# Weight tiles placed 256 bytes instead of 32 bytes off the activations' alignment in each SBUF partition

## What is computed

```python
u = rmsnorm(x, norm_mix) * (1.0 + scale1) + shift1
aq, ak, av, bq, bkv, biq, bik, biw, cq, ck, cv, g = split_cols(u @ w_in)
...
merged = gates[:, :, 0] * y_a + gates[:, :, 1] * y_b + gates[:, :, 2] * y_c
x = x + gate1 * (merged @ w_o)
u2 = rmsnorm(x, norm_mlp) * (1.0 + scale2) + shift2
h = jnp.square(jax.nn.relu(u2 @ w_ff1))
x = x + gate2 * (h @ w_ff2)
x = rmsnorm(x, norm_final)
for layer in range(2):
    proj = rms_norm(x, pre_norm[layer]) @ w_in_2[layer]
    ...
    mix = concatenate([y_conv, y_ret])
    x = x + rms_norm(mix @ w_out[layer], post_norm[layer])
```

## The kernel before

| tile | address | modulo 512 |
|---|---|---|
| u_hi, u_lo | 24704, 32896 | 128 |
| raw | 41088 | 128 |
| w_hi, w_lo | 73888, 90272 | 160 |
| h_hi, h_lo, mix_hi, mix_lo, m, oa, ob, oc | 146528 and on | 96 |

## Time and profile before

### The profile page before, as it was taken

How to read it: one execution, slowest core, us unless ns; L and a number is a source line. 1 busy time by engine, 2 the same in 40 slices (tenths; PEclk the granted TensorE clock), 3 DMA queues, 4 the chain that set the end, 5 groups by cost and what they waited for, 6 DMA issues and landing times.

```text
span 1012.1 us, 22089 instructions
## 1 busy us (share of the span) xinstructions
PE 971.3 (96%) x7850; PEld 946.8 (94%) x7850; DVE 611.2 (60%) x1032; ACT 493.8 (49%) x811; POOL 714.9 (71%) x902
## 2 busy tenths in 40 slices
PE   6998999999889999999999999999999999999997
PEld 6898889998889999999899999999989999999996
DVE  4889996656877554322555567764154666676612
ACT  3545557654446554454354446444435444644441
POOL 1585666668669888777466668998746666799873
PEclk9999999999999999999899999999999999999999
DMA  9984554646445547554244444455513444445521
GB/s 374 381 311 174 203 200 181 244 139 263 150 158 172 203 166 276 181 194 166 89 161 167 166 164 169 166 188 191 204 42 141 152 165 166 162 173 192 186 100 42
DMA packets 28226, 185.23 MB, mean 183 GB/s; under 512 B 3028, under 2 KB 5505, under 8 KB 6273
## 3 DMA queue, kind: packets, MB, share of 16 engines
q1 hardware_dynamic: 25832, 167.93, 46.2%
q10 hardware_dynamic: 2328, 16.40, 4.4%
HBM read 183.26 MB, written 1.07 MB: 182 GB/s over the span
## 4 chain that ended last, share of the span: by engine, by line
PE 82%; DVE 11%; issue 4%; ACT 2%; DMA 1%; POOL 0%; SPq 0%; POOLq 0%; DVEq 0%; ACTq 0%
PE mm L548 24%; PE mm L549 23%; PE mm L550 23%; PE mm L580 3%; DVE score L1573 1%; PE mm L566 1%; DVE w_lo L1382 1%; PE ps_s L877 1%; PE mm L567 1%; PE mm L568 1%; DVE ada_raw L1423 1%; PE ps_o L892 1%; PE ps_o L928 1%; DMA ident<-ident_d 1%; DVE merged L1720 1%
## 5 line engine op out<-in xcount | busy, mean ns | idle before, releaser
L464 POOL TENSOR_TENSOR w_lo<-raw,w_hi 128x256 fp32r<-128x256 f32 x876 | 700.1, 834 | 253.3 <-ACT w_hi L979 253.3
L548 PE MATMUL mm<-u_hi,w_hi 128*128 128x256 f32 x1608 | 464.3, 289 | 2.0 <-issue 1.8
L549 PE MATMUL mm<-u_lo,w_hi 128*128 128x256 f32 x1608 | 452.5, 281 | 0.0
L550 PE MATMUL mm<-u_hi,w_lo 128*128 128x256 f32 x1608 | 452.3, 281 | 0.0
L979 ACT ACTIVATE w_hi<-raw 128x1024 fp32r<-128x1024 f32 x291 | 308.2, 1059 | 165.7 <-PE mm L550 162.7
L548 PEld LDWEIGHTS mm<-u_hi,w_hi 128*128 128x128 f32 x1608 | 303.8, 189 | 8.4 <-issue 7.8
L549 PEld LDWEIGHTS mm<-u_lo,w_hi 128*128 128x128 f32 x1608 | 303.9, 189 | 2.0 <-issue 1.9
L550 PEld LDWEIGHTS mm<-u_hi,w_lo 128*128 128x128 f32 x1608 | 303.8, 189 | 0.0
L1382 DVE TENSOR_TENSOR w_lo<-raw,w_hi 128x1024 fp32r<-128x1024 f32 x72 | 96.9, 1346 | 117.8 <-ACT w_hi L979 116.1
L548 PE MATMUL mm<-mix_hi,w_hi 128*128 128x256 f32 x256 | 72.2, 282 | 0.4 <-DVE mix_lo L1957 0.4
L549 PE MATMUL mm<-mix_lo,w_hi 128*128 128x256 f32 x256 | 72.0, 281 | 0.0
(11 more groups left out here) (285 smaller groups left out, 1314.9 us busy)
## 6 DMA issues: line engine op xcount, KB each, us to landing
raw<-weights SPq DMA_DIRECT2D x145, 1024.0 KB, 4.8
ada_raw<-ada ACTq DMA_DIRECT2D x14, 1024.0 KB, 4.9
ada_raw<-ada SPq DMA_DIRECT2D x6, 1024.0 KB, 12.5
ada_more<-ada SPq DMA_DIRECT2D x4, 1024.0 KB, 12.6
bias<-tab_scratch SPq DMA_DIRECT2D x1, 1536.0 KB, 9.5
dec<-decay ACTq DMA_DIRECT2D x1, 1536.0 KB, 7.3
x<-xT SPq DMA_DIRECT2D x1, 1024.0 KB, 9.8
out<-x SPq DMA_DIRECT2D x4, 256.0 KB, 2.2
```

The source lines that it names most:

```text
L464: ins = nc.gpsimd.tensor_tensor(w_lo[:, s, at], r[:, at], hi[:, at], ALU.subtract)
L548: nc.tensor.matmul(dst, wh, rhs_hi(k), start=a, stop=False)
L549: nc.tensor.matmul(dst, wh, rhs_lo(k), start=False, stop=False)
L550: i = nc.tensor.matmul(dst, wl, rhs_hi(k), start=False, stop=b)
```

## The change

The two unused tiles step_w and step_vec get 64 columns instead of 8, that is 256 bytes instead of 32.

```diff
     raw = keep("raw", [P, RAW_PAIRS, 2 * KC * P])
-    keep("step_w", [P, 8])
+    keep("step_w", [P, 64])
     w_hi = keep("w_hi", [P, SLOTS, KC * P], F32R)
     w_lo = keep("w_lo", [P, SLOTS, KC * P], F32R)
-    keep("step_vec", [P, 8])
+    keep("step_vec", [P, 64])
     vec = keep("vec", [P, N_COLS])
```

## The result

| | us |
|---|---|
| before, median of 6 runs | 1009.33 (1007.19 to 1010.97) |
| after, median of 6 runs | 1018.38 (1015.86 to 1018.77) |
| ratio | 1.0089, 95% interval 1.0072 to 1.0107 |
| profiled execution after, its span | 1018.77, 1016.9 |

The forecast was 1010.8 us, no change. The time rose by 9.05 us; the new median, 1018.38, lies inside the range from 982 to 1037 and near the lower price of rival B (1019.4).

A forecast was written before the change was run, and what follows sets the result against it. TensorE was taken as the bound, matmuls times step; all terms were 0, so the profiled 1014.07 us, lying 3.25 above the median, gave 1010.8 us, range 982 to 1037.

The forecast's parts named there:

- rival B: Matmuls on u: reads meeting mid-matmul delay the next; +8.6 us (1019.4) or +25.3 (1036.1); chance 0.28, shared with slower GpSimd pieces.
- What bounds the kernel: TensorE: 6984 matmuls times the step between starts, 118.3 ns on u and 117.8 on the rest, 825 us.
- Part 1: All engines: no instruction is added, removed or moved; the sum contains no such term.
- part 5: Transfers: raw written at the same addresses, other loaded tiles shift by 448 bytes; term 0.
- Part 2: Weights against u, 32 to 256 bytes: step stays 118.3 ns, bounds 113.3 and 123.3; term 5064 x 0 = 0.
- Part 3: Weights against h, mix, m, oa, ob, oc, 64 to 352 bytes: step stays 117.8 ns, bounds 113.3 and 122.3.
- Part 4: Weights against raw, read by ScalarE, GpSimd and VectorE: GpSimd's pieces may grow 10% before TensorE waits; term 0.
- Rival A: Matmuls on u fall to 113.3 ns: -25.3 us, 985.5; if the others follow, 976.9; chance 0.30.
- Rival C: The matmul step does not depend on placement, the rhythms have another cause; 1010.8 us, sharing the forecast's chance of 0.42.

The follow-up runs named there:

- The map: Follow-up runs on the unchanged computation with weights at further distances past the moving operands, reading matmul steps; for example 1018.6 us with 0 past u, 128 past the others.
- the first two experiments: Against the kernel before: only step_w to 64 columns, 1012.09 us, ratio 1.0016; then only step_vec to 64 columns, 1012.75 us in a single run.
- the run with one: Kernel with weights 64 bytes past every moving operand, plus one extra warm-up matmul at each of eight places in the u stretches: 992.56 us, ratio 0.983.

## Why the prediction was wrong, step by step

- **What bounds the kernel** held: number of matmuls times step. The steps give +7.6 us, measured 7.3 to 10.8, and TensorE was not idle for longer. One reading in it was loose: the sum of 825 us, 82% of the span, was said to agree with the chain, but the chain's 82% are all lines of TensorE, and those of the 6984 matmuls are 73%.
- **Part 1** (no instruction moves) and **part 5** (transfers) held.
- **Part 2 is the step that failed.** The term for u was put at 0 and is 5064 x 1.67 = +8.5 us. The counts were good, and so was the lower bound; the upper one met the measured 120.0 by luck (see rival B). What failed was the reason for the choice. The argument said that both reads sweep a whole weight row in each matmul, so that the starting distance cannot matter to the cost. The map refutes it: 0, 32, 64 and 160 bytes give 120.0, 118.3, 113.3 or 117.8, and 120.0. Its premise, that load and matmul take about the same time, isn't in the rows either (0.19 against 0.28 us in the earlier trace rows). It was an argument without a row, and it outweighed the one row that spoke, two rhythms of the same matmul at one clock.
- The support that I drew from "32 against 64 is worth half a ns" was a misreading of the same kind: at 64 there are two rhythms, and the rows of the kernel before sat in the slower one nearly everywhere. The neighbour with its other rhythm was worth 5.0 ns.
- **Part 3:** put at 0, measured 117.3 on h and mix, -0.9 us; sign and size unimportant. That the others at 352 have a second rhythm of 118.7 was not seen in the changed kernel itself.
- **Part 4** held: raw alone changes neither the u step nor GpSimd's pieces (837 against 834 ns), and GpSimd takes 914 ns against 913 in the changed kernel.
- **Rival B** had the number, 120 ns and 1019.4 against 1018.38, at half of its 0.28. That the number fits is luck. Its price of 120 ns came from five steps in 0.60 us in the earlier trace rows, between starts given to 0.01 us; in ns the trace has 593 for the five, 118.6 each, with single steps of 116 to 122, so these five were no slower than the rest. Its mechanism, a meeting in the middle of the matmul that costs more than one at its start, isn't borne out: distance 0 costs the same 120.0 as 256, and 160 too.
- **Rival A** named the right stake at the wrong place: the faster rhythm does become the rule, at 64 bytes with a suitable entry, not at 256. **Rival C** fell with the first two experiments.
- The rule cited from the Trainium skill ("SBUF — State Buffer", section "Who interferes with whom": TensorE waits for nobody) would, as the prediction read it, leave all placements equal; the runs show 120.0 against 113.3 ns by placement and entry, so here the measurement decides. Whether one of the two reads waits is not shown.

**What stays open:** how the distance makes the rhythms. The runs show the period of 256 bytes, the numbers and their dependence on the entry; they don't show what inside the load or the matmul is held up. It wasn't tried whether the numbers change with another width of the moving operand. That the spread between executions of the kernel before (1003.64 to 1015.68 over all its runs) comes from different rhythms fits the two layers of the run with raw alone, but wasn't shown.

## What to carry to other kernels

When TensorE is the bound, read the step from the starts of successive matmuls in several undisturbed stretches, and compare it between operands and between stretches on the same operand: a spread of a few ns at full clock is a lever, here 1.5% of the time for 32 bytes of unused room. Place weights and moving operand by trying several distances and not by reasoning about them, and look at the step of each stretch, since a total can hide +8.5 and -8.6. Where one distance has two rhythms, what stands just ahead of a long stretch picks one for all of it.

## What the runs showed of the hardware

- The step of an fp32r matmul of 256 columns, with a new 128 x 128 load each, was 113.3 to 120.0 ns in long stretches at a granted clock of 1.00, and 123.3 in short pieces at distance 48, with nothing changed but addresses in the partition. The distance of the two operands sets which numbers occur, what stands ahead of a stretch which of them. In the three cases tried the numbers repeated after 256 bytes (0 and 256, 32 and 288, 96 and 352), and the pair at 64 came back at 320.
- At 64 and 192 two rhythms, 113.3 and 117.8, are each kept for hundreds of matmuls without a wait; so are 117.3 and 118.7 at 96, and 116.7 and 117.8 at 224. A single other matmul in between changed 117.8 to 113.3 in both layers of the run with one.
- The mean can hide uneven steps: in ns, single steps of the long u stretches at 118.3 ran from 115 to 123 in the kernel before, and all of those at 120.0 in the changed kernel took 120.
- The place of the weights in the partition and their distance to raw, which three engines read at the same time, left the u step at 118.3, in one run each.
